# Prompt attention: rows divided instead of diagonals, one mask over two banks, and the value products one step later

## The chip, the cores and the metric

One program runs on one core of a Trainium2 chip. A time is device microseconds from start to end of one execution. The core's engines have queues of their own: PE (TensorE, with its weight loads shown as PEld), DVE (VectorE), ACT (ScalarE), POOL (GpSimd) and SP (SyncE, which here issues the DMAs). They wait for each other by semaphores.

## The reference

The reference is one layer of a decoder, over a prompt of 2048 tokens and 32 sample tokens: RMSNorm, one projection, three groups of heads (A, B, C), output projection, MLP. The change is in the prompt's attention of groups A and B:

```
s = einsum(q, k) * hd ** -0.5;  s = where(mask, s, -inf)
m = max(s);  p = exp(s - m);  den = sum(p);  o = (p @ v) / den
A: 4 heads, keys at distance 0..128, and a sink per head: m = max(m, sink); den += exp(sink - m)
B: 6 heads, patterns (window, step) = (128,1), (512,4), (2048,16); outputs merged by their denominators
```

The merge of B's three patterns by their denominators is one softmax over all keys in which a key counts once for each pattern that has it; the kernel puts the logarithm of that count into the mask.

## The kernel before

`decoder_trunk` runs stages one after the other: project, prompt_attention, sample_attention, rwkv for prompt and sample, out_project, and the MLP in two halves. A stage begins when the one before it is done. The change lies in prompt_attention alone.

**Tiles.** A tile is one pair of heads u (0 and 1 of group A, 2 to 4 of group B) and 128 queries t (0 to 15), 80 tiles in all, numbered m; a row n = 2m + h is one head of it, 128 queries by its scores. Each has a "near" part, the keys of its own and the previous 128 positions, and in B a "far" part of f = t // 4 + 1 blocks of 128 keys, sorted by position modulo 4, so that each group of 32 queries of one class reads the keys of its class. So a row is 256 wide in A, and 384, 512, 640 or 768 wide in B, by fours of t (128 less at t = 0). Pool sorts queries and keys into that order (`sort`, lines 476 and 482).

**One tile through the engines.** PE `score` (lines 524 near, 534 far) writes PSUM banks of 512 columns, four in all: one bank a head up to 512 columns, else a near bank and a far bank a head. DVE `mask` (709) adds the mask, keeps the row's maximum and writes the row to SBUF; `bias` (725) turns the maximum into exp's bias. ACT `exp` (651) writes the probabilities `p_prob` and their sum. DVE `invert` (739) takes the reciprocal. Pool `scale` (489) multiplies a 128x128 identity by it: a diagonal matrix for each row. PE `turn` (556) multiplies each 128-column block by that diagonal, which transposes and divides it at once, into one of two PSUM banks `p_t`. A turn holds up to four blocks: the near one has both heads, far ones follow (one turn for f = 1 and 2, two for 3 and 4). `copy_turn` (DVE 733, ACT 659) copies turns to SBUF, even ones on DVE and odd ones on ACT. PE `near_v` (578) and, once in four tiles, `far_v` (592) multiply them by the values; ACT `copy_out` (665) takes the sum of four tiles to SBUF and SP stores it.

**The order** is written out by hand, each engine a loop over m. LAG is 2: in step m PE scores tile m and turns tile m - 2. Its value products wait in a list until the next turn has been issued, which in B is the far turn of the same tile:

```
turn(d, i)
for work in pending:
    work()
pending = []
if i == 0:
    pending.append(lambda d=d: near_v(d))
```

ACT does both exps of tile m before the copies of tile m - 2. DVE does masks, biases, reciprocals of tile m - 1, copies.

Of the kernel before, what the change touches and what calls it, by code (L numbers as in the profile page):

```python
# [9 lines left out]
ALU = mybir.AluOpType  # L10
# [307 lines left out]
def prompt_attention(nc, outer, projT, vtok, mask_w, mask_0, sinks, ident, mixT):  # L318
# [7 lines left out]
    banks = []  # L326
    for u, t in tiles:
        banks.append([(0, far(u, t) * P, width(u, t))] if width(u, t) <= 512 else
                     [(0, far(u, t) * P, far(u, t) * P), (far(u, t) * P, 0, width(u, t) - far(u, t) * P)])
    bank_before = [2 * sum(len(b) for b in banks[:m]) for m in range(NM + 1)]  # L330
# [9 lines left out]
    with ExitStack() as ctx:  # L340
# [17 lines left out]
        diag = s.sb("p2_diag", [P, PW, P])  # L358
# [3 lines left out]
        mx = s.sb("p2_mx", [P, 8, 2])  # L362
# [4 lines left out]
        sbank = [s.ps(f"p2_s{i}", [P, 512]) for i in range(NSB)]  # L367
# [16 lines left out]
        scaled = s.sem("p2_scaled")  # L384
# [23 lines left out]
        def _(sp):  # L408
# [5 lines left out]
            def load_k(u):  # L414
                if u >= 2:
                    sp.wait_ge(scored, bank_before[first(u - 1)])
# [52 lines left out]
        @block.gpsimd  # L469
        def _(pool):  # L470
            def sort(u, c):
                pool.wait_ge(q_in[c], 16 * (u + 1))
                if u >= 2 and c == 0:
                    pool.wait_ge(scored, bank_before[first(u - 1)])
# [19 lines left out]
            pool.wait_ge(consts_in, 64)  # L494
            for m in range(NM):
                u, t = tiles[m]
                for h in range(2):
                    scale(2 * m + h)
                if u + 1 < PAIRS and t % 3 == 2 and t > 2:
                    sort(u + 1, t // 3 - 1)  # L500

        @block.tensor
        def _(pe):
            def score(m):
# [10 lines left out]
                c = bank_before[m]  # L515
                split = len(banks[m]) == 2
                for h in range(2):
                    b = c + h
                    if b >= NSB:
                        pe.wait_ge(masked, b - NSB + 1)  # L520
                o = 0 if split else f * P
                for g in range(NCL):
                    for h in range(2):
                        mm = pe.matmul(sbank[(c + h) % NSB][cq(g), o:o + nn * P],
                                       q[u % 2][hp(h), t * P + CQ * g:t * P + CQ * (g + 1)],
                                       k[u % 2][hp(h), (t + 1 - nn) * P:(t + 1) * P], start=True, stop=True)
                        if g == NCL - 1 and (split or not f):
                            mm.then_inc(scored, 1)
                for g in range(NCL if f else 0):
                    for h in range(2):  # L530
                        b = c + h + (2 if split else 0)
                        if g == 0 and split:
                            pe.wait_ge(masked, b - NSB + 1)
                        mm = pe.matmul(sbank[b % NSB][cq(g), 0:f * P], q[u % 2][hp(h), t * P + CQ * g:t * P + CQ * (g + 1)],
# [4 lines left out]
            def turn(m, i):  # L539
# [3 lines left out]
                if i == 0:  # L543
                    pe.wait_ge(scaled, 2 * m + 2)
# [8 lines left out]
                for h in heads:  # L553
                    for c in chunks:
                        n = 2 * m + h
                        tr = pe.matmul(tbank[at % 2][:, j, :], prob[n % PW][:, 1 + c * P:1 + (c + 1) * P],  # L556
                                       diag[:, n % PW, :], start=True, stop=True)
# [41 lines left out]
            pending = []  # L599
            for m in range(NM + LAG):  # L600
                if m < NM:
                    score(m)
                if m >= LAG:
                    d = m - LAG
                    for i in range(len(turns[d])):
                        turn(d, i)
                        for work in pending:
                            work()
                        pending = []
                        if i == 0:  # L610
                            pending.append(lambda d=d: near_v(d))
                        if i and i == len(turns[d]) - 1 and d % NCL == NCL - 1:
                            pending.append(lambda d=d: far_v(d))
            for work in pending:
                work()
# [25 lines left out]
        def _(act):  # L641
# [11 lines left out]

            def copy_turn(m, i):
# [27 lines left out]
        def _(dve):  # L682
# [8 lines left out]
            def mask(m):  # L691
                u, t = tiles[m]
                c, f, w = bank_before[m], far(u, t), width(u, t)
                parts = banks[m][::-1]
                if m == first(A_PAIRS):
                    dve.wait_ge(mask_in, 16 * NCL)
                for i, (o, _, ww) in enumerate(parts):
                    for h in range(2):
                        n = 2 * m + h
                        b = c + 2 * i + h  # L700
                        if i == 0 and n >= RW:
                            dve.wait_ge(expd, n - RW + 1)
                        dve.wait_ge(scored, b + 1)
                        if t == 0:
                            mk = m0[:, 2 * P - w:2 * P]
                        else:
                            r = t % NCL if f else 0
                            mk = mw[:, r, (NCL - f) * P + o:(NCL - f) * P + o + ww]
                        dve.tensor_tensor_reduce(row[n % RW][:, 1 + o:1 + o + ww], sbank[b % NSB][:, 0:ww], mk,
                                                 1.0, -3.0e38, ALU.add, ALU.max, mx[:, n % 8, i:i + 1]).then_inc(masked, 1)  # L710

            def bias(n):
                m, h = divmod(n, 2)
                u, t = tiles[m]
                split = len(banks[m]) == 2
                dve.wait_ge(masked, bank_before[m] + (2 if split else 0) + h + 1)
                if n >= 8:
                    dve.wait_ge(expd, n - 7)
                if u < A_PAIRS:
                    other = sink8[:, 2 * u + h:2 * u + h + 1]  # L720
                elif split:
                    other = mx[:, n % 8, 1:2]
                else:
                    other = mx[:, n % 8, 0:1]
                dve.tensor_scalar(nb[:, n % 8:n % 8 + 1], mx[:, n % 8, 0:1], other, -SCALE,
                                  ALU.max, ALU.mult).then_inc(biased, 1)
# [8 lines left out]
            def invert(n):  # L735
                dve.wait_ge(expd, n + 1)
                if n >= 8:
                    dve.wait_ge(scaled, n - 7)
# [5 lines left out]
            for m in range(NM + LAG):  # L744
                if m < NM:
# [3 lines left out]
                    mask(m)  # L749
                    bias(2 * m)  # L750
                    bias(2 * m + 1)
# [3 lines left out]
                if m >= LAG:  # L755
                    d = m - LAG
                    for i in range(len(turns[d])):
                        copy_turn(d, i)
# [1584 lines left out]
```

## Time and profile before

| | us |
|---|---|
| median of 3 runs | 3822.87 (3814.53 to 3830.02) |
| the profiled execution | 3818.97 |
| its span, first to last instruction | 3817.2 |

| engine | busy, us | share |
|---|---|---|
| PE | 3302.7 | 87% |
| PEld | 2807.7 | 74% |
| DVE | 1621.6 | 42% |
| ACT | 910.0 | 24% |
| POOL | 253.6 | 7% |

The mean granted TensorE clock is 0.920 of full speed. The costliest groups of instructions are those of the projection and the MLP; the first of this stage is the turn (line 556): 1100 products, 160.5 us of PE busy time. Busy times are of the engine named, and several run at once, so they do not add up to the span.

### The profile page before, as it was taken

The numbers are of one execution on the slowest core, as the hardware profiler recorded it, in microseconds if no ns is written. First come the engines' busy times: TensorE is split into PE (matmuls) and PEld (weight loads), VectorE is DVE, ScalarE is ACT, GpSimd is POOL, SyncE is SP. The second block draws the span as 40 slices with busy tenths as digits, with TensorE's granted clock in tenths as the row PEclk, the third lists the DMA queues.
The fourth block names the chain that finished last, engine by engine and source line by source line (L and its number), as shares of the span: only waits on it lengthen the run. The fifth ranks groups of instructions, "written<-read, shape, count | busy, mean of one in ns | idle before, by whom it ended". The sixth has DMA issues, their size and how long they took to land. (4 is left out here: it accounts for less than half of the span.)

```text
span 3817.2 us, 66193 instructions
## 1 busy us (share of the span) xinstructions
PE 3302.7 (87%) x27354; PEld 2807.7 (74%) x27354; DVE 1621.6 (42%) x3168; ACT 910.0 (24%) x1636; POOL 253.6 (7%) x410
## 2 busy tenths in 40 slices
PE   5899999888695677777747978999999699999998
PEld 3899987566564667666635857888888598888887
DVE  3200001544312666666533334444444544444445
ACT  2211110544310333332112222112221222222222
POOL 0000000533100211121100000000000000000000
PEclk8999999999875888989857989999999899999999
DMA  2212121421151000000003553111210411111111
GB/s 91 76 69 69 69 74 54 131 72 43 64 195 57 17 21 22 21 22 21 11 26 123 173 182 105 44 44 44 66 44 34 173 45 45 44 44 44 44 44 57
DMA packets 142149, 250.42 MB, mean 66 GB/s; under 512 B 20352, under 2 KB 100352, under 8 KB 139112
## 3 DMA queue, kind: packets, MB, share of 16 engines
q1 hardware_dynamic: 141928, 247.24, 19.4%
q8 instruction: 167, 2.74, 0.3%
q14 instruction: 54, 0.44, 0.0%
HBM read 186.68 MB, written 60.52 MB: 65 GB/s over the span
## 5 line engine op out<-in xcount | busy, mean ns | idle before, releaser
L160 PE MATMUL p_bank<-p_xh,p_wh 128*128 128x416 f32 x800 | 286.1, 358 | 30.8 <-DVE p_xl L287 30.8
L161 PE MATMUL p_bank<-p_xl,p_wh 128*128 128x416 f32 x800 | 285.1, 356 | 0.0
L162 PE MATMUL p_bank<-p_xh,p_wl 128*128 128x416 f32 x800 | 284.0, 355 | 0.0
L2076 PE MATMUL mb_ub<-mb_hh,mb_wuh 128*128 128x352 f32 x768 | 251.5, 327 | 28.8 <-DVE mb_hl L2179 21.6
L2217 DVE TENSOR_TENSOR mb_y<-mb_y,mb_db 128x512 f32<-128x512 f32 (+1 forms) x288 | 197.4, 685 | 185.1 <-PE mb_db L2078 184.4
L2077 PE MATMUL mb_ub<-mb_hl,mb_wuh 128*128 128x352 f32 x768 | 248.4, 323 | 0.0
L2078 PE MATMUL mb_ub<-mb_hh,mb_wul 128*128 128x352 f32 x768 | 248.2, 323 | 0.0
L2217 DVE TENSOR_TENSOR ma_y<-ma_y,ma_db 128x512 f32<-128x512 f32 x256 | 175.8, 687 | 149.6 <-PE ma_db L2078 148.8
L2076 PE MATMUL mb_db<-mb_wdh,mb_uh 128*128 128x512 f32 (+1 forms) x576 | 228.1, 396 | 3.6 <-issue 3.6
L2078 PE MATMUL mb_db<-mb_wdh,mb_ul 128*128 128x512 f32 (+1 forms) x576 | 227.0, 394 | 0.0
L2077 PE MATMUL mb_db<-mb_wdl,mb_uh 128*128 128x512 f32 (+1 forms) x576 | 226.9, 394 | 0.0
L2076 PE MATMUL ma_ub<-ma_hh,ma_wuh 128*128 128x512 f32 x512 | 201.3, 393 | 27.3 <-DVE ma_hl L2179 17.2
L2076 PE MATMUL ma_db<-ma_wdh,ma_uh 128*128 128x512 f32 x512 | 200.0, 391 | 3.6 <-issue 3.6
L2077 PE MATMUL ma_ub<-ma_hl,ma_wuh 128*128 128x512 f32 x512 | 200.4, 391 | 0.0
L2078 PE MATMUL ma_ub<-ma_hh,ma_wul 128*128 128x512 f32 x512 | 200.4, 391 | 0.0
L2078 PE MATMUL ma_db<-ma_wdh,ma_ul 128*128 128x512 f32 x512 | 199.7, 390 | 0.0
L2077 PE MATMUL ma_db<-ma_wdl,ma_uh 128*128 128x512 f32 x512 | 199.6, 390 | 0.0
L556 PEld LDWEIGHTS p_t<-p_diag,p_prob 128*128 128x128 f32 x1100 | 137.9, 199 | 61.3 <-issue 35.5
L160 PEld LDWEIGHTS p_bank<-p_xh,p_wh 128*128 128x128 f32 x800 | 154.4, 193 | 35.1 <-DVE p_xl L287 33.8
L269 DVE TENSOR_TENSOR p_wl<-p_wr,p_wh 128x1024 fp32r<-128x1024 f32 x20 | 24.5, 1224 | 362.8 <-ACT p_wh L219 362.8
L556 PE MATMUL p_t<-p_diag,p_prob 128*128 128x128 f32 x1100 | 160.5, 295 | 13.0 <-POOL p_diag L489 12.7
L2076 PEld LDWEIGHTS mb_ub<-mb_hh,mb_wuh 128*128 128x128 f32 x768 | 145.9, 190 | 33.4 <-issue 20.5
(386 smaller groups left out, 6732.2 us busy)
## 6 DMA issues: line engine op xcount, KB each, us to landing
out_projT<-p_ob SPq DMA_DIRECT2D x100, 208.0 KB, 1.9
ma_wur<-w_up SPq DMA_DIRECT2D x32, 512.0 KB, 5.9
ma_wdr<-w_dn SPq DMA_DIRECT2D x32, 512.0 KB, 4.3
mb_wur<-w_up SPq DMA_DIRECT2D x32, 512.0 KB, 5.9
mb_wdr<-w_dn SPq DMA_DIRECT2D x32, 512.0 KB, 4.3
cp_z<-out_projT SPq DMA_DIRECT2D x8, 1408.0 KB, 8.1
p_kc<-kbT SPq DMA_DIRECT2D x8, 1344.0 KB, 6.1
p_vc<-vb SPq DMA_DIRECT2D x8, 1344.0 KB, 8.9
```

The costliest lines, as they stand in the source:

```text
L160: pe.matmul(out, wh_, mh, start=(k == 0), stop=False)
L161: pe.matmul(out, wh_, ml, start=False, stop=False)
L162: return pe.matmul(out, wl_, mh, start=False, stop=(k == KC - 1))
L269: dve.tensor_tensor(wl[j][:, :, :], wr[:, :, :], wh[j][:, :, :].bitcast(F32), ALU.subtract).then_inc(w_low, 1)
L556: tr = pe.matmul(tbank[at % 2][:, j, :], prob[n % PW][:, 1 + c * P:1 + (c + 1) * P], diag[:, n % PW, :], start=True, stop=True)
L2076: pe.matmul(out, wh, mh, start=first, stop=False)
L2077: pe.matmul(out, wh, ml, start=False, stop=False)
L2078: return pe.matmul(out, wl, mh, start=False, stop=last)
L2217: dve.tensor_tensor(ys, ys, db[b % ND][0:n, :], ALU.add).then_inc(y_added, 1)
```

## The change

The five edits go together.

- `scale` no longer makes diagonals. The rows of probabilities themselves are multiplied by the reciprocal, in place: head 0's on ACT (after the exps of the next tile), head 1's on Pool. `turn` becomes PE's transpose against the identity.
- The four score banks become one PSUM tensor. A row wider than 512 has its far part at the end of one bank and its near part at the start of the next, so that one mask instruction covers both, and there is one maximum a row. Both banks of a head are freed by that mask.
- `near_v` and `far_v` of a tile run one step later, after the near turn of the next tile.
- ACT does the copies of tile m - 2 and the output copy ahead of the exps of tile m.
- DVE does head 0's mask, the reciprocals, the near copy, head 1's mask, the biases, the other copies.

```diff
@@ Pool
-            def scale(n):
+            def scale(m):
+                n, w = 2 * m + 1, width(*tiles[m])
                 pool.wait_ge(inverted, n + 1)
-                if n >= PW:
-                    pool.wait_ge(turned, turn_before[(n - PW) // 2 + 1])
-                pool.tensor_scalar(diag[:, n % PW, :], idt[:, :], rec[:, n % 8:n % 8 + 1], None,
-                                   ALU.mult).then_inc(scaled, 1)
+                pool.tensor_scalar(prob[n % PW][:, 1:1 + w], prob[n % PW][:, 1:1 + w], rec[:, n % 8:n % 8 + 1], None,
+                                   ALU.mult).then_inc(scaled[1], 1)
@@ PE: score
-                    b = c + h
-                    if b >= NSB:
-                        pe.wait_ge(masked, b - NSB + 1)
-                o = 0 if split else f * P
+                    if bank(h) >= NSB:
+                        pe.wait_ge(masked, owner[bank(h) + nbanks(u, t) - 1 - NSB] + 1)
+                o = 0 if two else f * P
...
-                        if g == NCL - 1 and (split or not f):
+                        if g == NCL - 1 and not f:
                             mm.then_inc(scored, 1)
+                o = 512 - f * P if two else 0
@@ PE: turn
-                    pe.wait_ge(scaled, 2 * m + 2)
+                    for h in range(2):
+                        pe.wait_ge(scaled[h], m + 1)
...
-                        tr = pe.matmul(tbank[at % 2][:, j, :], prob[n % PW][:, 1 + c * P:1 + (c + 1) * P],
-                                       diag[:, n % PW, :], start=True, stop=True)
+                        tr = pe.transpose(tbank[at % 2][:, j, :], prob[(2 * m + h) % PW][:, 1 + c * P:1 + (c + 1) * P], idt[:, :])
@@ PE: the loop (the list of pending work goes)
+            for m in range(NM + LAG + 1):
                 if m < NM:
                     score(m)
+                d = m - LAG
+                if 0 <= d < NM:
+                    turn(d, 0)
+                if d > 0:
+                    near_v(d - 1)
+                for i in range(1, len(turns[d]) if 0 <= d < NM else 0):
+                    turn(d, i)
+                if d > 0 and d % NCL == 0 and tiles[d - 1][0] >= A_PAIRS:
+                    far_v(d - 1)
@@ ACT
+            def scale(m):
+                n, w = 2 * m, width(*tiles[m])
+                act.wait_ge(inverted, n + 1)
+                act.activation(prob[n % PW][:, 1:1 + w], prob[n % PW][:, 1:1 + w], ACT.Copy,
+                               scale=rec[:, n % 8:n % 8 + 1]).then_inc(scaled[0], 1)
...
             for m in range(NM + LAG):
+                d = m - LAG
+                for i in range(len(turns[d]) if d >= 0 else 0):
+                    copy_turn(d, i)
+                if d > NCL and d % NCL == 1:
+                    copy_out(d // NCL - 1)
                 if m < NM:
                     exp(2 * m)
                     exp(2 * m + 1)
-                if m >= LAG:
-                    d = m - LAG
-                    for i in range(len(turns[d])):
-                        copy_turn(d, i)
-                        if i == 0 and d % NCL == 0 and d:
-                            copy_out(d // NCL - 1)
+                if 1 <= m <= NM:
+                    scale(m - 1)
@@ DVE: mask(n), and the loop
+                dve.wait_ge(scored, n + 1)
...
+                o = 512 - f * P if nbanks(u, t) == 2 else 0
+                dve.tensor_tensor_reduce(row[n % RW][:, 1:1 + w],
+                                         sbank[:, b:b + nbanks(u, t), :].rearrange("p b c -> p (b c)")[:, o:o + w], mk,
+                                         1.0, -3.0e38, ALU.add, ALU.max, mx[:, n % 8:n % 8 + 1]).then_inc(masked, 1)
...
-                    mask(m)
-                    bias(2 * m)
-                    bias(2 * m + 1)
+                    mask(2 * m)
                 if 1 <= m <= NM:
                     invert(2 * m - 2)
                     invert(2 * m - 1)
-                if m >= LAG:
-                    d = m - LAG
-                    for i in range(len(turns[d])):
-                        copy_turn(d, i)
+                if d >= 0:
+                    copy_turn(d, 0)
+                if m < NM:
+                    mask(2 * m + 1)
+                    bias(2 * m)
+                    bias(2 * m + 1)
+                for i in range(1, len(turns[d]) if d >= 0 else 0):
+                    copy_turn(d, i)
```

## Rows read from the trace of the kernel before

**Rows 1.** Stretches: length, busy (count) of PE, PEld, DVE, ACT, POOL, clock, DMA, GB/s.

```profile
835.69:856.35 20.66, 18.63 (x289) 15.44 (x288) 8.49 (x37) 8.77 (x23) 4.75 (x8) 0.96 0.13 40
856.35:873.92 17.57, 14.91 (x235) 11.10 (x233) 9.26 (x36) 8.11 (x22) 6.88 (x10) 1.00 0.77 226
873.92:895.42 21.50, 18.81 (x267) 13.90 (x265) 11.44 (x53) 10.20 (x23) 6.92 (x10) 1.00 0.04 14
895.42:926.69 31.27, 26.17 (x297) 17.80 (x296) 13.63 (x54) 11.78 (x23) 9.01 (x12) 0.88 0.03 10
676.93:749.44 72.51, 65.21 (x886) 43.89 (x885) 41.77 (x243) 43.15 (x132) 43.81 (x66) 0.98 0.48 138
```

**Rows 2.** Waits of 751 to 1028 us: us in total, times, longest.

```profile
PE p_o L578 <- ACT p_ptn L659: 21.6, 11, 2.3
```

**Rows 3.** Timeline of a 768-wide tile of B: start, us, engine, line, operation [idle before].

```profile
902.49 0.66 PE L524 MATMUL p_s<-p_k,p_q 64*32 64x256 f32 x16
904.11 0.69 DVE L709 CUSTOM_DVE_ANT_0 p_row<-p_s,p_mask_w 128x512 f32<-128x512 f32 x1
...
905.58 0.94 ACT L651 ACTIVATE p_prob<-p_row,p_nb 128x768 f32<-128x768 f32 x1 [3.47 <-DVE p_nb L725]
...
907.43 0.57 ACT L659 ACTIVATE p_ptn<-p_t 128x512 f32<-128x512 f32 x1
...
908.06 0.66 PE L578 MATMUL p_o<-p_ptn,p_v 128*64 128x128 f32 x8 [2.28 <-ACT p_ptn L659]
...
913.66 2.84 PE L592 MATMUL p_o<-p_ptf,p_vc 128*64 128x128 f32 x48
```

**Rows 4.** Timeline of two tiles of A.

```profile
690.44 0.66 PE L524 MATMUL p_s<-p_k,p_q 64*32 64x256 f32 x16
...
691.03 0.97 PEld L556 LDWEIGHTS p_t<-p_diag,p_prob 128*128 128x128 f32 x8 [0.41 <-POOL p_diag L489]
...
691.30 0.43 DVE L709 CUSTOM_DVE_ANT_0 p_row<-p_s,p_mask_w 128x256 f32<-128x256 f32 x1 [1.55 <-PE p_s L524]
...
692.00 0.33 DVE L725 TENSOR_SCALAR p_nb<-p_mx,p_sink 128x1 f32<-128x1 f32 x2
...
692.12 0.66 PE L578 MATMUL p_o<-p_ptn,p_v 128*64 128x128 f32 x8
692.24 0.51 ACT L651 ACTIVATE p_prob<-p_row,p_nb 128x257 f32<-128x257 f32 x1 [1.13 <-DVE p_nb L725]
...
692.50 1.19 POOL L489 TENSOR_SCALAR p_diag<-p_ident,p_rec 128x128 f32<-128x128 f32 x2 [1.52 <-DVE p_rec L739]
...
692.71 0.66 PE L524 MATMUL p_s<-p_k,p_q 64*32 64x256 f32 x16
...
695.41 0.66 PE L524 MATMUL p_s<-p_k,p_q 64*32 64x256 f32 x16
```

**Rows 5.** Turns here and transposes in the output projection: a group, then timeline.

```profile
L556 PE MATMUL p_t<-p_diag,p_prob 128*128 128x128 f32 x1100 | 160.5, 295 | 13.0 <-POOL p_diag L489 12.7
...
2080.09 1.04 PE L1890 MATMUL p_tp<-p_ident,p_xn 128*128 128x128 f32 x8
...
2080.88 0.48 PE L1903 MATMUL p_acc<-p_wh,p_mh 128*128 128x512 f32 x1
```

**Rows 6.** Groups of ACT: busy us, mean ns, idle before.

```profile
L1938 ACT ACTIVATE p_xn<-p_x,p_stat 128x1024 f32<-128x1024 f32 x16 | 18.4, 1152 | 3.7 <-DVE p_stat L1977 3.7
L665 ACT ACTIVATE p_mo<-p_o 128x512 f32<-128x512 f32 x20 | 21.8, 1088 | 8.8 <-PE p_o L592 8.3 <-PE p_o L578 0.5
```

**Rows 7.** Groups of Pool.

```profile
L489 POOL TENSOR_SCALAR p_diag<-p_ident,p_rec 128x128 f32<-128x128 f32 x160 | 94.9, 606 | 214.4 <-DVE p_rec L739 210.3 <-PE p_t L556 3.9
L476 POOL COPY p_q<-p_qr 128x512 f32<-128x512 f32 x20 | 22.3, 1116 | 669.8 <-DMA p_qr<-out_projT 669.8
```

**Rows 8.** Two neighbouring stretches about 895 us, columns as in Rows 1.

```profile
892.00:895.40 3.40, 1.44 (x15) 1.16 (x14) 0.56 (x1) 1.91 (x5) 1.14 (x2) 1.00 0.02 5
895.40:898.80 3.40, 3.40 (x36) 1.30 (x36) 1.26 (x5) 0.49 (x1) 0.00 (x0) 0.50 0.00 0
```

More of the change, by code:

```diff
@@ L324, in prompt_attention @@
     width = lambda u, t: P * (far(u, t) + near(t))
[L326 to L330, printed above, removed]
+    nbanks = lambda u, t: 1 if width(u, t) <= 512 else 2
+    bank_before, owner = [0], []
+    for m, (u, t) in enumerate(tiles):
+        owner += [2 * m + h for h in range(2) for _ in range(nbanks(u, t))]
+        bank_before.append(len(owner))
     turns, turn_before = [], [0]
@@ L366, in prompt_attention @@
         NSB = 4
-        sbank = [s.ps(f"p2_s{i}", [P, 512]) for i in range(NSB)]
+        sbank = s.ps("p2_s", [P, NSB, 512])
         tbank = [s.ps(f"p2_t{i}", [P, 4, P]) for i in range(2)]
@@ L383, in prompt_attention @@
         inverted = s.sem("p2_inverted")
-        scaled = s.sem("p2_scaled")
+        scaled = [s.sem(f"p2_scaled{h}") for h in range(2)]
         turned = s.sem("p2_turned")
@@ L415, in load_k @@
                 if u >= 2:
-                    sp.wait_ge(scored, bank_before[first(u - 1)])
+                    sp.wait_ge(scored, 2 * first(u - 1))
                     if u - 2 >= A_PAIRS:
@@ L473, in sort @@
                 if u >= 2 and c == 0:
-                    pool.wait_ge(scored, bank_before[first(u - 1)])
+                    pool.wait_ge(scored, 2 * first(u - 1))
                 part = slice(NCL * c, NCL * (c + 1))
@@ L483, in sort @@
                                      k[u % 2][:, :].rearrange("p (s g) -> p g s", g=NCL)[:, :, ks]).then_inc(k_sorted, 1)
-            def scale(n):
+            def scale(m):
+                n, w = 2 * m + 1, width(*tiles[m])
                 pool.wait_ge(inverted, n + 1)
-                if n >= PW:
-                    pool.wait_ge(turned, turn_before[(n - PW) // 2 + 1])
-                pool.tensor_scalar(diag[:, n % PW, :], idt[:, :], rec[:, n % 8:n % 8 + 1], None,
-                                   ALU.mult).then_inc(scaled, 1)
+                pool.tensor_scalar(prob[n % PW][:, 1:1 + w], prob[n % PW][:, 1:1 + w], rec[:, n % 8:n % 8 + 1], None,
+                                   ALU.mult).then_inc(scaled[1], 1)
             for c in range(NCL):
                 sort(0, c)
-            pool.wait_ge(consts_in, 64)
             for m in range(NM):
                 u, t = tiles[m]
-                for h in range(2):
-                    scale(2 * m + h)
+                scale(m)
                 if u + 1 < PAIRS and t % 3 == 2 and t > 2:
@@ L598, in _ @@
             pe.wait_ge(consts_in, 64)
-            pending = []
-            for m in range(NM + LAG):
+            for m in range(NM + LAG + 1):
                 if m < NM:
                     score(m)
-                if m >= LAG:
-                    d = m - LAG
-                    for i in range(len(turns[d])):
[L606 to L615, printed above, removed]
+                d = m - LAG
[7 more added lines that the diff above has]
+                    far_v(d - 1)
         def turn_copy(m, i, engine):
@@ L689, in sinks_of @@
                 z.then_inc(sunk, 1)
[L691 to L710, printed above, removed]
@@ L712, in bias, with mask @@
-            def bias(n):
+            def mask(n):
                 m, h = divmod(n, 2)
                 u, t = tiles[m]
-                split = len(banks[m]) == 2
-                dve.wait_ge(masked, bank_before[m] + (2 if split else 0) + h + 1)
+                f, w = far(u, t), width(u, t)
+                if n == 2 * first(A_PAIRS):
+                    dve.wait_ge(mask_in, 16 * NCL)
+                b = (bank_before[m] + nbanks(u, t) * h) % NSB
+                if n >= RW:
+                    dve.wait_ge(expd, n - RW + 1)
+                dve.wait_ge(scored, n + 1)
+                if t == 0:
+                    mk = m0[:, 2 * P - w:2 * P]
+                else:
+                    r = t % NCL if f else 0
+                    mk = mw[:, r, (NCL - f) * P:(NCL - f) * P + w]
+                o = 512 - f * P if nbanks(u, t) == 2 else 0
+                dve.tensor_tensor_reduce(row[n % RW][:, 1:1 + w],
+                                         sbank[:, b:b + nbanks(u, t), :].rearrange("p b c -> p (b c)")[:, o:o + w], mk,
+                                         1.0, -3.0e38, ALU.add, ALU.max, mx[:, n % 8:n % 8 + 1]).then_inc(masked, 1)
@@ L717, in bias @@
+            def bias(n):
+                u, t = tiles[n // 2]
+                dve.wait_ge(masked, n + 1)
                 if n >= 8:
                     dve.wait_ge(expd, n - 7)
[L719 to L726, printed above, removed]
+                top = mx[:, n % 8:n % 8 + 1]
+                other = sink8[:, 2 * u + n % 2:2 * u + n % 2 + 1] if u < A_PAIRS else top
+                dve.tensor_scalar(nb[:, n % 8:n % 8 + 1], top, other, -SCALE, ALU.max, ALU.mult).then_inc(biased, 1)
@@ L737, in invert @@
                 if n >= 8:
-                    dve.wait_ge(scaled, n - 7)
+                    dve.wait_ge(scaled[n % 2], n // 2 - 3)
                 dve.reciprocal(rec[:, n % 8:n % 8 + 1], den[:, n % 8:n % 8 + 1]).then_inc(inverted, 1)
@@ L744, in _ @@
             for m in range(NM + LAG):
+                d = m - LAG
                 if m < NM:
```

20 lines of the change are left out of this document (7 added, 13 removed).

## The prediction, made before the changed kernel ran

> **What bounds the kernel now.** I began with the span cut by stretches [rows 1]. The prompt attention runs from about 669 to 1028 us, some 360 of 3817 us, and nothing outside it is edited. It has two parts: 32 tiles of group A (256 scores wide), and three pairs of group B of 16 tiles each, whose width goes 384, 512, 640, 768 by fours. For one B pair the four groups take 20.66, 17.57, 21.50 and 31.27 us: 91.0 us. TensorE (PE) is busy 86 to 91% of them, so I asked next what its gaps wait for. In B the name is the copy of the turned near block: 21.6 us of PE waiting for ACT alone [rows 2]. The timeline shows how [rows 3]. In a 768-wide tile ACT starts its exps 3.09 us after the scores and copies the near block only behind them (907.43), and PE stands 2.28 us before the value products. The 768-wide tiles take 31.27 / 4 = 7.8 us each.
>
> In A the loop is another [rows 4]: scores at 690.44, mask at 691.30, bias at 692.00, the two diagonals of Pool from 692.50 (1.19 us), then the turn that multiplies by them, then the value products; the score at 695.41 is two tiles on, 4.97 us later. The 28 tiles from 676.93 take 72.51 us, 2.59 each (some meet a sort of Pool's).
>
> **The change, part by part.**
>
> *Transposes for products.* A turn is 550 products, each of two PE records (1100 records) [rows 5]; eight records hold PE for 1.09 us (691.03 to 692.12) [rows 4]. The transpose used in the output projection is one record, and eight of them release PE after 0.79 us [rows 5]: 0.10 each against 0.27 for a product. Per near block of four: 0.45 instead of 1.09. In all 550 x 0.17 = 94 us less PE work; only what lies in a binding loop becomes time.
>
> *The scale moves onto the rows.* Pool's diagonal (0.606 us for 128 columns) goes. Head 1's row is scaled on Pool, head 0's on ACT. ACT's price: 1.152 us for 1024 columns with a per-row scale [rows 6], less 0.84 ns a column (the exps of 257 and 768 columns take 0.51 and 0.94 us [rows 3, 4]), so 0.51 for 256 and 0.94 for 768. It runs behind the next tile's exps. Pool's price for wide rows is not in the trace: the low end is the 512-column sort, 2.18 ns a column (1.7 us for 768), the high end the diagonal's 4.7 ns (3.6 us) [rows 7]. I take 2.9, nearer to the same operation. Pool starts after the reciprocal, about 2.7 us after the scores, and ends at 4.4 to 6.3, ahead of ACT's scale at about 7, so neither end moves the sum. A sort pair (2 x 1.12) behind it would at the high end delay 4 tiles of 16 by under 1 us: 0 to +8 us in all. The Trainium skill ("GPSIMD Engine Reference", section 3.1) gives 1.8 cycles an element at best and 2.6 for two inputs; by that 768 columns are 1.2 to 1.7 us, below my value, and the diagonal's 606 ns is far above what 128 elements would cost by it, so the row decides here.
>
> *One mask over two banks.* Two instructions (256 and 512 wide, 0.43 and 0.69) become one. Issued back to back they hold DVE 0.35 and 0.61; one of 768 holds 0.88. This saves 0.08 a head, but the near mask can no longer start before the far scores: 904.11 is 1.62 us after the scores [rows 3], where a near mask starts after 0.86 [rows 4]. 48 fewer instructions; net zero to a loss of 0.5 us a tile, kept in the loop below. The next scores now wait for both masks (all four banks are used), 1.62 + 0.88 + 0.2 + 0.96 + 0.1 = 3.8 us, or 4.4 with a copy between: below the loop.
>
> *Value products one step later, copies ahead.* The 2.28 us waits go: the near copy has a whole tile of time. What is late next is the row scale. The new loop goes over two tiles: scores, both masks, bias, both exps, ACT's scale of the tile before, that tile's turn, the value products, and then the scores of two tiles on.
>
> A (256), each term from [rows 4] unless named: scores to mask 0.86; two masks 0.70; reciprocals between them 0.17; bias to exp 0.24; DVE's copy of 512 columns in every second tile 0.60; exps 1.00 (2 x 0.51, overlapping); scale 0.51; hand-over 0.08; turn 0.45; value products 0.59. That is 4.6 without the copy and 5.2 with it; in one tile of four ACT's output copy (1.09 [rows 6]) delays the exps by 0.9. Mean 5.1 for two tiles, 2.57 each, against 2.59 now. So A gains nothing: Pool's 1.19 and the longer turn are traded for exps and scale.
>
> B at 768 [rows 3]: scores to mask 1.62; masks 1.76; reciprocals and bias 0.41; here ACT first finishes the copy of the last turn (0.57 at 907.43, ends about 4.25), so the exps start at 4.3; exps 1.85; scale 0.94; 0.08; three turns 1.35 with gaps 0.2, value products 0.59. Sum 9.3, or 4.65 a tile. Between the ends, by width: 6.2, 7.2 and 8.25 for 384, 512, 640 (an estimate from these two sums). Once in four tiles the far value products stand in one of the two interleaved loops, 2.84 us for 48 records [rows 3], so 16f records are 0.95f; they belong to the group before. And ACT's output copy adds about 0.8. Four tiles are two loops plus these: 12.4 + 3.8 + 0.8 + 1.2 (the first two turns are still wide) = 18.2; 14.4 + 0.95 + 0.8 = 16.2; 16.5 + 1.9 + 0.8 = 19.2; 18.6 + 2.85 + 0.8 = 22.3. A pair: 75.9 against 91.0, 15 us less, of which 9 in the 768 group. Three pairs: I take 14.5 each, since the first has no wide far products before it: 43.5 us.
>
> *The clock.* The rows show the cost that stands against this. After a stretch in which PE was busy 1.44 of 3.40 us the granted clock fell from 1.00 (2.4 GHz) to 0.50 (1.2 GHz) [rows 8]. The change takes 94 us of PE work out and leaves PE waiting on a loop, so such dips become more frequent: in A PE's records would cover 0.66 + 0.60 + 0.66 less overlap, about 1.75 of 2.57 us (68%, now 90%). At half clock the PE part of A's loop doubles (0.86 + 1.04 of 5.1, +37%: 27 us over A), and a B pair becomes PE-bound. Its work at full clock: scores 16 x 1.07 (0.59 in A and, from 0.86 against 1.62, 0.19 a far block, 2.5 of them in the mean), turns 16 x 0.45 + 80 x 0.10 + gaps of 1.6, value products 16 x 0.59, far ones 0.95 x 10: 17.1 + 16.8 + 9.4 + 9.5 = 53 us, so 106 at half, 15 over now. All of the stage at half clock costs 43.5 + 27 + 45 = 115 us against all at full. I take 13% of the stage newly at half clock: +15 us. The bounds are 0% and 60%. Sum: -43.5 + 15 = -28 us. The Trainium skill ("TensorE: Matmul & The Clock Gate", Part 4: PE-mode transpose) says that transpose mode does not count as PE being busy for the gate; this trace has transposes only between dense products, so it cannot tell. What such a mechanism does here is the first rival.
>
> The profiled execution took 3818.97 us, 3.9 below the median of 3822.87, so -28 is 3791 against its own time and 3795 against the median, which I give.
>
> **The rivals.**
>
> *The clock stays down (slower).* If the gate does not see transposes, PE's visible work in A is 1.3 of 2.57 us, 51%, close to the 42% after which it fell. The deciding point: the 43.5 us are used up when 38% of the stage (43.5/115) is at half clock, a mean granted clock of 0.81. At 60% it is -43.5 + 69 = +25: 3848. For: the dips came in waits, and A will have one in each tile. Against: in the stretch at half clock PE was busy throughout [rows 8], since the same work then takes twice as long; in the B groups outside 768 the mean clock is 0.96 to 1.00 [rows 1], so dips end soon and a share over one half is hard to hold. 6%.
>
> *The clock takes most (no change).* A share of about 30%: -43.5 + 34.5 = -9: 3814. 15%. It is the same mechanism, short of its deciding point.
>
> *The row scale is dearer (no change).* Scale, hand-overs and sorts lengthen each B loop by 10% (23 us of 228): -43.5 + 23 + 8 = -12: 3811. For: ACT gets 80 more instructions and stands in-order behind copies that wait for PE. Against: ACT's sum for a pair stays near 50 us. 9%.
>
> *The loop is shorter than I add up (faster).* If tiles overlap where I put terms in a row, the pair falls toward its PE work, 54 plus drain, say 66: 3 x 25 = -75, +15 for the clock: 3763. 12%.
>
> **How the numbers follow.** My own case 58%, of which 6 fall within the 0.5% (19 us) that a measurement of this kernel can tell from no change. Faster 52 + 12 = 64%, same 6 + 15 + 9 = 30%, slower 6%. Range 3768 to 3822: from most of the shorter loop's case to the two cases of no change; it leaves out the slow one and the far end of the fast one.
>
> **What would show each step.** Turn records 550, near 0.27 us, with the PE released after about 0.10 each. A near 72 us for its 28 tiles. The 768-wide group near 22 us, with no wait of PE for a near copy over 1 us but waits of the turn for ACT's scaled row. Pool's 768-wide scale between 1.7 and 3.6 us. Mean granted clock of the stage near 0.90 (now 0.96 over [rows 1]). Wrong: if PE's waits for the scaled row are absent (the loop is not what binds), if the A part changes by over 8 us at full clock, or if the clock is below 0.81.

## The result, and the profile of the changed kernel

The changed kernel takes 3835.16 us (median of 18 runs), the kernel before 3822.55 (also 18 runs): a ratio of 1.0035, interval 1.0025 to 1.0045. It is slower by 12.6 us, a third of a percent, which puts it 40 us above the forecast and outside its range. The profiled execution took 3832.23 us, its span is 3829.7.

All of it lies in the prompt attention. Its last output copy starts at 1041.12 us, where it started at 1028.23 before, and what follows is as long as it was. The stretches, in the columns of [rows 1]: tiles 4 to 31 of A, the second B pair by its groups of four tiles, and the last pair with the drain.

```profile
680.99:775.19 94.20, 63.08 (x780) 33.72 (x778) 44.83 (x242) 53.26 (x161) 36.66 (x39) 0.83 0.36 99
...
851.79:873.02 21.23, 15.43 (x255) 11.38 (x255) 8.72 (x38) 11.35 (x26) 8.19 (x7) 0.92 0.04 14
873.02:891.64 18.62, 13.46 (x205) 7.80 (x205) 10.66 (x41) 10.64 (x26) 9.10 (x7) 0.91 0.82 239
891.64:911.91 20.27, 14.75 (x228) 9.41 (x229) 10.46 (x37) 12.72 (x27) 8.43 (x6) 1.00 0.05 16
911.91:934.97 23.06, 17.21 (x253) 11.04 (x253) 12.27 (x38) 14.79 (x27) 10.64 (x7) 1.00 0.04 14
934.97:1042.00 107.03, 81.11 (x1051) 54.48 (x1050) 45.44 (x158) 57.12 (x116) 33.05 (x20) 0.82 0.04 14
```

The pair that took 91.0 us takes 83.2, with 8 us from its 768-wide group (31.27 to 23.06 [rows 1]). But A, forecast as unchanged, goes from 71.2 us for these 28 tiles (72.5 in [rows 1], which begins about one tile earlier) to 94.2, or 3.36 a tile.

The waits of the stage (us in total, times, longest) say what for. PE's wait for the near copy [rows 2] is gone. Instead the turn waits for ACT's row scale, and both copying engines wait for the turn.

```profile
PE p_t L552 <- ACT p_prob L647: 97.0, 67, 4.2
...
ACT p_ptf L655 <- PE p_t L552: 92.2, 48, 3.7
...
DVE p_ptn L722 <- PE p_t L552: 45.3, 46, 1.8
...
ACT p_ptn L655 <- PE p_t L552: 28.4, 28, 1.9
```

The timeline of one A tile closes the circle (columns of [rows 3], to be read beside [rows 4]):

```profile
695.55 0.50 ACT L647 ACTIVATE p_prob<-p_prob,p_rec 128x256 f32<-128x256 f32 x1
...
696.11 0.66 PE L552 MATMUL p_t<-p_ident,p_prob 128*128 128x128 f32 x4 [1.73 <-ACT p_prob L647]
696.69 0.42 PEld L573 LDWEIGHTS p_o<-p_ptn,p_v 128*64 128x64 f32 x8 [0.17 <-issue]
...
696.80 0.69 DVE L722 COPY p_ptn<-p_t 128x512 f32<-128x512 f32 x1 [0.95 <-PE p_t L552]
...
697.41 0.42 DVE L704 CUSTOM_DVE_ANT_0 p_row<-p_s,p_mask_w 128x256 f32<-128x256 f32 x1
...
697.75 0.33 DVE L715 TENSOR_SCALAR p_nb<-p_mx,p_sink 128x1 f32<-128x1 f32 x2
697.99 0.51 ACT L641 ACTIVATE p_prob<-p_row,p_nb 128x257 f32<-128x257 f32 x1 [1.94 <-DVE p_nb L715]
...
698.50 0.49 ACT L641 ACTIVATE p_prob<-p_row,p_nb 128x257 f32<-128x257 f32 x1
...
698.99 0.49 ACT L647 ACTIVATE p_prob<-p_prob,p_rec 128x256 f32<-128x256 f32 x1
...
699.54 0.66 PE L552 MATMUL p_t<-p_ident,p_prob 128*128 128x128 f32 x4 [1.60 <-ACT p_prob L647]
```

The turn of tile m-2 at 696.11 releases DVE's copy (0.69 later). The copy holds back head 1's mask of tile m (0.61), and with it the bias (0.34) and the exps (0.24 to the start, 1.00 for both). Behind the exps, in ACT's order, stands the scale of tile m-1, for which the next turn waits (0.55). The sum is 3.43 us. Where ACT has the copy, it stands ahead of the exps itself: 0.70 + 0.49 + 1.00 + 0.55 = 2.74, and 3.57 with an output copy. Of four tiles two take the first length, one the second and one the third: 3.29 in the mean, 92 us for 28 tiles, all at full clock.

The trace has these lengths at full clock. From the scale at 685.85 to the one at 708.70 are seven tiles, 3.26 us each, and the granted clock is 1.00 throughout:

```profile
685.85:708.70 22.85, 12.85 (x196) 7.12 (x196) 11.68 (x62) 14.05 (x42) 8.68 (x9) 1.00 0.44 85
```

### The profile page after: what moved, and what is told of

It reads as the page before. It is cut to its first block and busy times, and to the rows that moved or that the text cites. A ratio compares the mean times of both kernels' runs of the same rounds, so it can differ in the third digit from the quotient of the medians.

```text
span 3829.7 us, 64845 instructions
## 1 busy us (share of the span) xinstructions
PE 3261.4 (85%) x26804; PEld 2747.6 (72%) x26804; DVE 1624.5 (42%) x3072; ACT 952.9 (25%) x1716; POOL 270.0 (7%) x330
## 5 line engine op out<-in xcount | busy, mean ns | idle before, releaser
L552 PE MATMUL p_t<-p_ident,p_prob 128*128 128x128 f32 x550 | 103.1, 321 | 100.6 <-ACT p_prob L647 97.0
L552 PEld LDWEIGHTS p_t<-p_ident,p_prob 128*128 128x128 f32 x550 | 68.1, 159 | 159.8 <-ACT p_prob L647 147.1
```

The lines of the kernel that those rows point to most:

```text
L552: tr = pe.transpose(tbank[at % 2][:, j, :], prob[(2 * m + h) % PW][:, 1 + c * P:1 + (c + 1) * P], idt[:, :])
```

## The experiments

**Theory 1** is that circle. **Theory 2**: the lower clock costs the time. **Theory 3**: scaling rows loads ACT and Pool too much. In the table "A" is tiles 4 to 31 with their granted clock, "B" the first and second B pair, "last" the third pair with the drain, in us, all from one profiled execution each (those of e5 and e10 are 9 and 8 us above their medians). Each ratio is to runs of the kernel before that were taken with it. "Two back" and "three back" are the distance of the turn from the scores, LAG in the code.

| kernel | median us | ratio to before | A (clock) | B | last |
|---|---|---|---|---|---|
| before | 3822.6 | 1 | 71.2 (1.00) | 84.0, 91.0 | 102.6 |
| changed | 3835.2 | 1.0035 (1.0025 to 1.0045) | 94.2 (0.83) | 76.6, 83.2 | 107.2 |
| e1 turn three back | 3739.9 | 0.9787 (0.977 to 0.9804) | 68.3 (0.93) | 60.5, 65.3 | 78.4 |
| e2 and reciprocals last | 3723.8 | 0.9736 (0.9719 to 0.9752) | 61.5 (0.92) | 56.3, 61.8 | 74.9 |
| e3 products by identity | 3897.7 | 1.0195 (1.0178 to 1.0212) | 108.9 (0.88) | 93.1, 102.0 | 122.4 |
| e4 diagonals | 3785.2 | 0.9899 (0.9882 to 0.9915) | 73.6 (0.97) | 68.4, 76.4 | 90.8 |
| e5 diagonals on e2 | 3771.4 | 0.986 (0.9843 to 0.9876) | 70.2 (0.93) | 64.8, 74.4 | 91.0 |
| e6 scale first | 3758.7 | 0.983 (0.9814 to 0.9847) | 68.6 (0.95) | 62.5, 69.4 | 85.8 |
| e7 copies behind | 3801.4 | 0.9935 (0.9917 to 0.9954) | 70.4 (0.92) | 77.1, 84.0 | 94.7 |
| e8 before, three back | 3812.7 | 0.9964 (0.9948 to 0.998) | 70.5 (0.93) | 76.6, 89.4 | 104.3 |
| e9 two masks on e2 | 3721.7 | 0.973 (0.9714 to 0.9747) | 63.4 (0.91) | 54.0, 61.1 | 73.5 |
| e10 values same step on e2 | 3735.2 | 0.9759 (0.9743 to 0.9775) | 62.3 (0.91) | 58.2, 66.0 | 81.1 |
| e11 e6 and reciprocals last | 3778.9 | 0.9871 (0.9852 to 0.9889) | 78.2 (0.97) | 65.8, 72.0 | 87.5 |
| e12 early loads on e2 | 3722.8 | 0.974 (0.9726 to 0.9753) | 56.0 (0.96) | 55.1, 61.8 | 74.9 |

**e6, the scale first.** The smallest edit against the circle: one call of ACT moves.

```diff
+                if 1 <= m <= NM:
+                    scale(m - 1)
                 if m < NM:
                     exp(2 * m)
                     exp(2 * m + 1)
-                if 1 <= m <= NM:
-                    scale(m - 1)
```

> Changed kernel (turn two tiles back), ACT's scale of tile m-1 ahead of the exps of tile m instead of behind them. The copies stay ahead. Theory 1: the scale leaves the closed loop of copy, mask, exps, scale, turn; what is left is DVE's chain exps, reciprocals, copy, mask, bias, exps, 3.2 us with DVE's near copy and 2.5 without: 28 tiles of A in 74 to 82 us, a B pair in 70 to 76, the whole 45 to 60 us below the changed kernel, near 3783. Theory 3: the scale's load is the same, so the time too. Theory 2: clock and time as in the changed kernel.

It is 76 us faster than the changed kernel, with the same instructions. In the timeline the scale (700.29) now stands ahead of the exps (701.70), and the turn starts when Pool's scale of the other head ends (700.68 + 0.93 = 701.61), though the profile names ACT.

```profile
700.29 0.50 ACT L647 ACTIVATE p_prob<-p_prob,p_rec 128x256 f32<-128x256 f32 x1
700.42 0.16 DVE L728 RECIPROCAL p_rec<-p_den 128x1 f32<-128x1 f32 x1 [0.33 <-ACT p_prob L641]
700.50 0.69 DVE L722 COPY p_ptn<-p_t 128x512 f32<-128x512 f32 x1
...
700.68 0.93 POOL L487 TENSOR_SCALAR p_prob<-p_prob,p_rec 128x256 f32<-128x256 f32 x1 [1.78 <-DVE p_rec L728]
701.11 0.41 DVE L704 CUSTOM_DVE_ANT_0 p_row<-p_s,p_mask_w 128x256 f32<-128x256 f32 x1
...
701.68 0.42 PEld L552 LDWEIGHTS p_t<-p_ident,p_prob 128*128 128x128 f32 x4 [0.86 <-ACT p_prob L647]
701.70 0.51 ACT L641 ACTIVATE p_prob<-p_row,p_nb 128x257 f32<-128x257 f32 x1 [0.90 <-DVE p_nb L715]
...
702.20 0.50 ACT L641 ACTIVATE p_prob<-p_row,p_nb 128x257 f32<-128x257 f32 x1
...
702.82 0.16 DVE L728 RECIPROCAL p_rec<-p_den 128x1 f32<-128x1 f32 x1 [0.33 <-ACT p_prob L641]
```

It came out 24 us below the 3783 expected, outside the range. My sum of DVE's chain had the copy twice (its 0.69, and the 0.61 for which it holds DVE): from one second reciprocal to the next the chain is 2.40 us, not 3.2. The trace has 47 full near copies on DVE, so the term is worth at most 0.69 x 47 = 32 us by my estimate, which covers the 24.

**e7, the copies behind.** The other way to open the circle: ACT goes exps, scale, copies; DVE masks, biases, reciprocals, copies.

```diff
@@ ACT
-                for i in range(len(turns[d]) if d >= 0 else 0):
-                    copy_turn(d, i)
...
                 if 1 <= m <= NM:
                     scale(m - 1)
+                for i in range(len(turns[d]) if d >= 0 else 0):
+                    copy_turn(d, i)
...
@@ DVE
                     mask(2 * m)
+                    mask(2 * m + 1)
+                    bias(2 * m)
+                    bias(2 * m + 1)
                 if 1 <= m <= NM:
                     invert(2 * m - 2)
                     invert(2 * m - 1)
-                if d >= 0:
-                    copy_turn(d, 0)
...
-                for i in range(1, len(turns[d]) if d >= 0 else 0):
+                for i in range(len(turns[d]) if d >= 0 else 0):
                     copy_turn(d, i)
```

> Changed kernel (turn two tiles back) with the order of the kernel before on ACT and DVE: ACT does exps, scale, then the copies and the output copy; DVE both masks, the biases, the reciprocals, then the copies. Theory 1: in A the copies no longer stand in the loop, which goes over two tiles again (4.6 to 5.1 us): 28 tiles in 64 to 73 us (94 now). In B the far turns have only two PSUM banks, and a copy behind the exps and the scale holds the next turn up in the same tile: the pairs do not get shorter, those 640 and 768 wide up to 2 us a tile longer. The whole between 25 us less and 20 us more than the changed kernel. Theories 2 and 3: A stays above 88.

A is 70.4 us, as the loop over two tiles gave it. The first two B pairs are no shorter than in the changed kernel (77.1 and 84.0 us), and the 768-wide group of the second takes 31.2 us. Both are as expected, and so is the reason: the waits show the turn waiting for ACT's near copy, which now stands behind the exps and the scale.

```profile
PE p_t L552 <- ACT p_ptn L655: 35.1, 11, 3.8
```

The whole came out 34 us below the changed kernel, 9 more than the far end given. The 384- and 512-wide groups lost their circle too (17.6 and 14.1 us in the second pair against 21.2 and 18.6), which I had not counted. In the second pair the 768-wide group takes that back. The last pair keeps its gain and is 12.5 us shorter (94.7 against 107.2).

**e1 and e2, the turn one tile further back.** What the turn needs should then be done when it comes. e2 also moves the reciprocals.

```diff
-LAG = 2
+LAG = 3
-        RW, PW = 4, 6
+        RW, PW = 4, 8
@@ DVE, e2 alone
-                if 1 <= m <= NM:
-                    invert(2 * m - 2)
-                    invert(2 * m - 1)
...
                     bias(2 * m + 1)
+                if 1 <= m <= NM:
+                    invert(2 * m - 2)
+                    invert(2 * m - 1)
```

> Changed kernel with the turn three tiles behind the scores (LAG 3) and eight buffers of probabilities; every instruction and its order on each engine stay. Theory 1 (the copies that now stand ahead of head 1's mask and of the exps wait for a turn, and the turn waits for ACT's row scale, the last ACT work of the step before, so that one tile is one closed loop of 3.3 us): the turn of three back finds its rows scaled, PE's waits for the scaled row (97 us now) fall below 30, and what is left is DVE's chain exps, reciprocals 0.3, copy 0.69 in every second tile, mask 0.61, bias 0.34, start 0.24, exps 1.0: 28 tiles of A take 72 to 84 us (95 now), a B pair 68 to 76 (83 now), the whole 40 to 55 us less than the changed kernel, near 3785. Theory 2 (the lower granted clock of transposes sets the time): A stays above 90 at a clock of 0.82 or less, the whole within 15 us of the changed kernel. Theory 3 (the row scaling loads ACT and Pool too much): the load is the same, so the whole stays within 15 us too.

> As the kernel before it (turn three tiles back), and DVE's two reciprocals of tile m-1 stand behind the biases of tile m instead of behind head 0's mask. Theory 1: this opens the last closed loop of one tile (exps m-1, reciprocals, copy, mask, bias, exps m); ACT's own work sets the pace, exps 1.0 + scale 0.5 + copy 0.5 in every second tile + output copy 1.17 in every fourth: 28 tiles of A in 58 to 68 us, a B pair in 62 to 70, the whole 70 to 90 us below the changed kernel, near 3755. Theory 2: no faster than the kernel with three back, clock below 0.8. Theory 3: within 15 us of the changed kernel.

They are 95 and 111 us faster than the changed kernel. PE's wait for the scaled row falls from 97.0 us to 11.6 (e1) and 4.5 (e2). Three lines of e2 follow: that wait, A, and the second B pair, which PE now fills (58.27 of 61.79 us) at full clock.

```profile
PE p_t L552 <- ACT p_prob L647: 4.5, 6, 0.9
```

```profile
674.64:736.17 61.53, 52.45 (x774) 29.26 (x774) 41.19 (x236) 50.10 (x156) 35.59 (x38) 0.92 0.57 163
...
792.48:854.27 61.79, 58.27 (x941) 38.15 (x939) 40.39 (x148) 48.99 (x105) 35.86 (x25) 1.00 0.29 87
```

ACT and Pool scale the same rows as in the changed kernel, so theory 3 as I put it falls here. e1 came out 40 us beyond its range and e2 21. For e1, A and the first two pairs are 3 to 8 us each below what I gave, for which the double counting stands, and the last pair, on which I had put nothing, is 29 us shorter. For e2 I had ACT as the pace; in B it is PE.

**e3, a product for the transpose.**

```diff
-  tr = pe.transpose(tbank[at % 2][:, j, :], prob[...][...], idt[:, :])
+  tr = pe.matmul(tbank[at % 2][:, j, :], prob[...][...], idt[:, :], start=True, stop=True)
```

> Changed kernel, the turn as a product by the identity instead of PE's transpose; nothing else. Eight records of about 0.13 us instead of four transposes of 0.10 in each near turn, 550 turns in all. Theory 1: the turn stands in the closed loop, so the longer turn adds about 0.55 us to each tile: 28 tiles of A take 103 to 112 us, the whole 30 to 70 us more, whatever the clock does. Theory 2 (transposes are not counted as work by the clock gate): the clock of A rises from 0.81 to 0.95 or more and A falls below 92 us.

It is as theory 1 has it: A takes 108.9 us, and the whole 62.5 us more than the changed kernel. Theory 2 wanted A below 92. The clock of A is 0.88, not 0.95, and that of the last pair 0.92; in the changed kernel they are 0.83 and 0.82. The clock rose and the time rose with it.

**e4 and e5, diagonals again**, once on the changed kernel and once on e2.

```diff
-                n, w = 2 * m + 1, width(*tiles[m])
...
-                pool.tensor_scalar(prob[n % PW][:, 1:1 + w], prob[n % PW][:, 1:1 + w], rec[:, n % 8:n % 8 + 1], None, ...
+                for h in range(2):
...
+                    pool.tensor_scalar(diag[:, n % PW, :], idt[:, :], rec[:, n % 8:n % 8 + 1], None, ...
@@ PE: the turn is pe.matmul(..., prob block, diag[:, n % PW, :]); ACT has no scale
```

> Changed kernel with the row scaling alone undone: Pool makes a diagonal for both heads of a tile again, the turn multiplies by it, and neither Pool nor ACT touches the rows. The orders, the one mask over two banks and the value products one step later stay. Theory 1 (the loop through ACT's scale and the copies ahead): ACT's scale leaves the loop, 28 tiles of A fall to 73 to 81 us; in B PE has 0.17 us more for each of the blocks and ACT 0.5 to 0.9 us a tile less, a pair 80 to 90 us; the whole within 20 us of the changed kernel. Theory 3 (row scaling is what costs): A at or below its 72.5 us of the kernel before and the whole faster than the kernel before. Theory 2: the clock is back at 0.95 and A is at 73 to 80.

> The kernel with the turn three tiles back and the reciprocals last, and Pool's diagonals for both heads in place of the scaled rows (turns are products by a diagonal again). What differs from the three-back kernel with the reciprocals last (3723.78) is the row scaling alone, this time with nothing waiting for it. Theory 1 (row scaling costs time only where the turn waits for it): PE sets the pace and has longer turns, 0.17 us for each block, so this is slower than the row-scaling one: a B pair 75 to 78 us (62 there), 28 tiles of A 66 to 71, the whole near 3775, about the 3785 of the diagonals two tiles back. Theory 3 (scaling rows loads ACT and Pool too much): as fast as 3724 or faster.

e4 alone speaks for theory 3 as much as for theory 1: with diagonals the changed kernel is 50 us faster, where I had given 20. A is in its range (73.6), and B below the 80 to 90 given (68.4 and 76.4). e5 decides: where nothing waits for the scale, the scaled rows are 48 us faster than the diagonals (3723.8 against 3771.4), since PE is the bound and the diagonals fill it. PE is busy without a gap there:

```profile
812.71:887.10 74.39, 74.39 (x1083) 57.02 (x1081) 41.73 (x148) 38.16 (x88) 27.67 (x41) 1.00 0.24 73
```

So the row scaling is a gain of 48 us that its place inside the circle turns into a loss of 50. The pair also bears on the clock: transposes (e2) and products (e5) of otherwise equal kernels show the same one, 0.92 and 0.93 in A and 1.00 in all B pairs. Against theory 2, that the clock costs the time in A, stand e3 and the seven tiles at full clock above.

**e8, the distance alone, in the kernel before** (the same two lines as e1).

> The kernel before with the turn three tiles back and eight buffers of probabilities and diagonals, nothing else. Its own waits are for the near copy, which stands behind the exps of the same step however far back the turn is, and in A it is near its PE work (64 of 71 us). Theory 1: little to gain, 28 tiles of A 67 to 71, B pairs as they were within 3 us, the whole 0 to 15 us less than the kernel before; the 95 us of the three-back kernel come from the distance together with the changed parts. If instead the distance alone is what counts, this gains 60 us or more.

It gains 11 us, within the 0 to 15 expected: PE still waits for ACT's near copy (17.8 us from 700 us on, 21.6 before [rows 2]). The gain of e1 needs both the changed parts and the distance. One term was off: the first B pair is 7 us shorter, not within 3.

**e9 and e10, two parts of the change undone on e2**: the split mask with its four banks, and the old places of the value products.

```diff
@@ e9, DVE (score, banks and bias as in the kernel before)
-                    mask(2 * m)
+                    mask(m, [0])
...
-                    mask(2 * m + 1)
+                    mask(m, [1, 2, 3])
@@ e10, PE: the loop of the kernel before, with its list of pending work
```

> The kernel with the turn three tiles back and the reciprocals last (3723.78), with the one mask over two banks undone: rows wider than 512 again have a near and a far bank, two mask instructions and two maxima, and the near mask can start before the far scores are there. 48 more instructions of DVE, no other change. Theory: PE sets the pace of the B pairs (58 of 62 us busy), so DVE's instructions are beside the path: within 5 us of 3724. A rival: the next near scores had to wait for a whole mask and now go earlier, or DVE's 0.08 us a head counts: more than 8 us either way, all of it in the 640 and 768 wide groups (16.8 and 18.5 us in the second B pair).

> The kernel with the turn three tiles back and the reciprocals last (3723.78), with the value products back where the kernel before had them: in B behind the far turn of the same tile, in A (as before too) behind the near turn of the next one. Theory: in B PE waits for the near copy again, 0.3 to 1.5 us a tile, less than the 2.3 of the kernel before because the copy no longer stands behind the exps: the three pairs 15 to 60 us longer together, A within 3 us, the whole 3740 to 3780. If the copies ahead alone had made the gain, it stays within 5 us of 3724.

The one mask is worth nothing here (3721.7 against 3723.8). The value products one step later are worth some 11 us (3735.2 against 3723.8). In the profiles the three pairs are 12.3 us longer without it, under the 15 to 60 expected, with PE waiting 16.2 us for DVE's near copy:

```profile
PE p_o L573 <- DVE p_ptn L727: 16.2, 23, 0.9
```

**e11, both orders at once, two back.**

> Changed kernel (turn two tiles back, six buffers), with ACT's scale of tile m-1 ahead of the exps of tile m and DVE's reciprocals behind the biases: both closed loops of one tile opened by order alone. Theory 1: ACT waits 0.3 us for the reciprocals behind its exps in each tile, A 2.1 to 2.4 us a tile, 28 in 60 to 67, a B pair 62 to 67, the whole 3725 to 3745, so the third step of distance was only one way to open the loop. Against it: if the distance itself matters, it stays near the 3759 of the scale first alone.

This was a miss: 3778.9 us, 20 slower than e6. With the scale ahead of the exps, the reciprocal that it needs must not stand behind the biases of the next tile. There it waits for copy, mask and bias, ACT waits for it, and the exps wait behind that. It is a new circle, which I had not drawn:

```profile
690.67 0.51 ACT L647 ACTIVATE p_prob<-p_prob,p_rec 128x256 f32<-128x256 f32 x1 [1.18 <-DVE p_rec L728]
```

**e12, the next pair's queries and keys ahead of the last store.**

```diff
...
             for u in range(PAIRS):
...
                 for c in range(NCL):
+                    if u + 2 < PAIRS and c == NCL - 1:
+                        load_qk(u + 2)
                     store(NCL * u + c)
...
```

> The kernel with the turn three tiles back and the reciprocals last (3723.78), and one change of order on SP: the queries and keys of the next pair are loaded ahead of the last store of a pair, not behind it. In the trace of that kernel Pool stands 4.9 us in a sort that waits for these keys (714.7 to 719.6), head 1's row scale stands behind it, PE's next turn comes 5.8 us late, and the granted clock of the A part is 0.92. Theory: the load leaves SP up to 10 us earlier, the wait goes and with it most of the half-clock time after it: 28 tiles of A in 50 to 58 us instead of 61.5, the whole 4 to 12 us less, 3712 to 3720. Against: the transfer itself (keys and values of one pair share the queues) is what is late, and nothing changes.

The wait goes as expected, and the gain is not there. A takes 56.0 us instead of 61.5, without Pool's wait of 4.9, but the whole is the same as e2 (a ratio of 0.974 against 0.9736), not the 3712 to 3720 us given. In this profile the stage's first load began 5.8 us later than in e2's, behind the stage ahead of it, which no edit touches. Whether the 5.5 us are lost there or inside the spread of these runs stays open.

## Why the prediction was wrong

**The step that failed** is "The new loop goes over two tiles", and with it "So A gains nothing". I had the copy as 0.60 us more of DVE, as though its turn were done. In the new order the copy stands ahead of work of tile m and waits for a turn, which waits for ACT's last instruction of the step before. That makes a loop of one tile: 3.29 us, not 2.57. Its cost in A is 23 us. e6 shows that it is the loop: the same work with the scale one place earlier gives A 68.6.

**The 40 us** between forecast and result are made up so: A is 23 us longer where I had no change, and the three pairs are 7, 7 and 19 us short of the 14.5 each that I gave them. Together that is 56 us. It leaves 41 when the 15 that I had set aside for the clock are taken off, since these lengths already hold what the clock cost.

**B's sum** had the same fault, smaller. For the groups of the second pair the forecast was 18.2, 16.2, 19.2 and 22.3 us, and they measured 21.2, 18.6, 20.3 and 23.1. At 768 the two-tile sum (9.3 for two) was near the truth, since the circle at 0.69 + 0.61 + 0.87 + 0.25 + 1.85 + 0.98 = 5.25 (near copy, its hold on DVE, mask, start, exps, scale and hand-over; the output copy comes on top) is not much longer than 4.65; at 384 and 512 the forecast was 3.0 and 2.4 us short a group. The first two pairs gained 7.4 and 7.8 us of the 14.5 forecast.

**The clock** was sized about right: it went from 0.95 to 0.87 over the stage, where I gave 0.90. In A it did not decide, since the circle alone is 92 of the 94 us at full clock. In the last pair it may have taken most of the gain (102.6 to 107.2 us at 0.82): there the 384-, 512- and 640-wide groups take 64.6 us against 60.1 in the second pair, at a clock of 0.84, 0.83 and 0.78 against 0.92, 0.91 and 1.00. What the clock alone costs there was not isolated.

```profile
934.97:956.70 21.73, 16.51 (x256) 11.98 (x255) 8.77 (x38) 11.35 (x26) 8.20 (x7) 0.84 0.04 14
956.70:976.50 19.80, 14.76 (x205) 9.01 (x205) 10.56 (x41) 10.83 (x26) 6.60 (x5) 0.83 0.04 14
976.50:999.54 23.04, 18.60 (x228) 11.21 (x229) 10.46 (x37) 12.73 (x27) 6.43 (x5) 0.78 0.04 13
```

So slower came true, to which I gave 6%, but not by the mechanism that I gave it for: the mean clock stayed above its deciding point of 0.81.

The Trainium skill ("TensorE: Matmul & The Clock Gate", Part 4: PE-mode transpose) says that a transpose does not count as PE being busy in the same way. With the pipeline open no run shows an effect on the clock: e2 and e5 are level, in loops where products stand between the transposes. With it closed this stays open: e3 has 0.88 and 0.92 in A and the last pair where the changed kernel has 0.83 and 0.82, but its longer turns also give PE more work.

**Single terms.** PE's share of the four groups in [rows 1] is 84 to 90%, not the "86 to 91%" of the text; no sum uses it. Pool's 768-wide scale is 2.2 us (2.9 taken, bounds 1.7 to 3.6), ACT's 0.50 and 0.92 (0.51 and 0.94). A near turn holds PE for 0.58 us (696.11 to the value products at 696.69), not the 0.45 worked out from the eight transposes of [rows 5]. In e2 a pair's PE work is 58.3 us where I had 53, which hid nothing here.

**What it had in sight.** The text named its own disproof, A changing by over 8 us at full clock, and "Scale, hand-overs and sorts lengthen each B loop by 10%" was the rival nearest the truth. That rival named ACT, which "stands in-order behind copies that wait for PE", but I did not follow that to the turn.

## What to carry to other kernels

When an in-order engine gets a copy ahead of new work, ask what the copy's producer waits for; if that is this engine's last instruction of the step before, or leads to it through another queue, the pipeline has shrunk to one step. Draw every such circle, those over one step and those over two, and count the one that takes longest per step. Open it with the cheapest means, an exchange of two calls (76 us here) or one more step of distance with its buffers (95), draw the circles again for the new order (e11), and judge the other parts only afterwards: the row scaling was a loss of 50 us inside the circle and a gain of 48 outside it.

## What the runs showed of the hardware that I had not expected

Pool's multiplication by a value per row took these times, read from its groups (busy, mean ns, idle):

```profile
L487 POOL TENSOR_SCALAR p_prob<-p_prob,p_rec 128x256 f32<-128x256 f32 x33 | 30.5, 925 | 70.9 <-DVE p_rec L728 70.9
...
L487 POOL TENSOR_SCALAR p_prob<-p_prob,p_rec 128x768 f32<-128x768 f32 x12 | 26.5, 2205 | 36.9 <-DVE p_rec L728 36.7
...
L704 DVE CUSTOM_DVE_ANT_0 p_row<-p_s,p_mask_w 128x768 f32<-128x768 f32 x24 | 22.8, 952 | 21.9 <-PE p_s L529 21.9
```

This is (2205 - 925) / 512 = 2.5 ns a column and some 0.29 us fixed. By that estimate about half of the diagonal's 606 ns for 128 columns was fixed cost, and a wide row costs less than that figure scaled up. The mask that reads two PSUM banks took 952 ns for 768 columns, less than the two instructions it replaces (0.43 + 0.69, [rows 3, 4]). And a clock that had fallen stayed down although PE was then busy. In the drain of the changed kernel PE was busy 6.62 of 10.10 us at 2.4 GHz and then 8.85 of 10.20 us at 1.2 GHz, three times the 3.4 us of the dip in [rows 8]:

```profile
1017.00:1027.10 10.10, 6.62 (x102) 4.78 (x100) 4.17 (x16) 7.17 (x14) 2.21 (x1) 1.00 0.08 28
```

```profile
1027.10:1037.30 10.20, 8.85 (x48) 6.74 (x48) 2.09 (x4) 3.26 (x5) 2.20 (x1) 0.50 0.01 2
```
